# The adaLN modulation as fp32 products with the weights stationary, spread over the first norm and the mLSTM stages

## The reference, cut to what matters

```python
def trunk_layer(x, cond, li, P, rope, ctx):
    mod = jax.nn.silu(cond) @ P['w_mod'][li] + P['b_mod'][li]      # (1024) @ (1024 x 6144)
    sh1, sc1, g1, sh2, sc2, g2 = jnp.split(mod[:, None, :], 6, axis=-1)
    h = rms_norm(x, P['norm1'][li]) * (1 + sc1) + sh1
    mo, new_ctx = even_mixer(...) if li % 2 == 0 else odd_mixer(...)
    x = x + g1 * mo
    h = rms_norm(x, P['norm2'][li]) * (1 + sc2) + sh2
    x = x + g2 * swiglu(h, P['w_ffn_in'][li], P['w_ffn_out'][li])
```

## Time and profile before

| | us |
|---|---|
| runs | 3986.44, 3990.02, 3990.70 |
| median | 3990.02 |
| span of the profiled execution (no other time was kept of it) | 3988.1 |
| busy: TensorE, VectorE, ScalarE, GpSimd | 3424, 1966, 1161, 1820 |
| modulation | 8.9 to 159.2 |
| first norm, up to the first product of the projection | 159.2 to 206.3 |
| projection | 206.3 to 578.9 |
| gates | 578.9 to 642.0 |
| query and key stage | 642.0 to 679.2 |
| scan | 679.2 to 820.4 |
| output stage | 820.4 to 854.0 |
| all that follows | 854.0 to 3988 |

### The profile page before, as it was taken

One profiled execution on the slowest core, in us unless ns is written; L12 is line 12 of the kernel. 1 busy time (PEld: TensorE's weight loads), 2 busy tenths in 40 slices (PEclk: granted clock), 3 DMA queues, 4 the chain that ended last, 5 costly groups with the idle time before them and its releaser, 6 DMA issues. The chain is left out here.

```text
span 3988.1 us, 52620 instructions
## 1 busy us (share of the span) xinstructions
PE 3424.4 (86%) x17646; PEld 2961.2 (74%) x17646; DVE 1966.0 (49%) x3464; ACT 1161.0 (29%) x2474; POOL 1820.2 (46%) x1700
## 2 busy tenths in 40 slices
PE   7789993647768799999999686888888799999998
PEld 2377873536666699999998574777777699999998
DVE  7764115677772433333333675888883433333333
ACT  5611001146650310110110313888870310110110
POOL 0053102536551245545545354888871245545545
PEclk9899996859998899999999796999999899999999
DMA  8612212020002111110110212000002110110111
GB/s 331 253 69 98 87 45 77 5 94 17 15 7 90 50 44 34 53 42 32 53 42 1 103 61 78 17 16 16 18 1 90 53 43 32 53 42 32 53 42 48
DMA packets 118990, 232.74 MB, mean 58 GB/s; under 512 B 64064, under 2 KB 71360, under 8 KB 108736
## 3 DMA queue, kind: packets, MB, share of 16 engines
q1 hardware_dynamic: 118880, 231.33, 17.0%
HBM read 197.74 MB, written 34.34 MB: 58 GB/s over the span
## 5 line engine op out<-in xcount | busy, mean ns | idle before, releaser
L812 POOL TENSOR_TENSOR x<-x,ff_gated 128x512 f32<-128x512 f32 x396 | 512.1, 1293 | 320.1 <-DVE ff_gated L897 296.6
L806 POOL TENSOR_TENSOR ff_lo<-ff_raw,ff_hi 128x1024 fp32r<-128x1024 f32 x132 | 329.0, 2499 | 547.2 <-ACT ff_hi L773 547.0
L897 DVE TENSOR_TENSOR ff_gated<-ff_y_banks,gate_tokens 128x512 f32<-128x512 f32 x396 | 273.8, 691 | 412.6 <-PE ff_y_banks L871 411.2
L610 PE MATMUL tile_sum<-w_hi,tokens_hi 128*128 128x512 f32 x1008 | 405.1, 402 | 68.5 <-DVE w_lo L641 45.0
L773 ACT ACTIVATE ff_hi<-ff_raw 128x1024 fp32r<-128x1024 f32 x132 | 137.9, 1061 | 1118.7 <-PE ff_y_banks L871 720.5
L886 DVE TENSOR_TENSOR ff_silu<-ff_silu,ff_up_banks 128x384 f32<-128x384 f32 x132 | 72.5, 550 | 718.2 <-PE ff_up_banks L842 718.2
L611 PE MATMUL tile_sum<-w_lo,tokens_hi 128*128 128x512 f32 x1008 | 403.0, 400 | 0.0
L612 PE MATMUL tile_sum<-w_hi,tokens_lo 128*128 128x512 f32 x1008 | 402.3, 399 | 0.0
L838 PE MATMUL ff_gate_banks<-tokens_hi,ff_hi 128*128 128x384 f32 x1056 | 354.6, 336 | 19.4 <-POOL ff_lo L806 19.4
L839 PE MATMUL ff_gate_banks<-tokens_lo,ff_hi 128*128 128x384 f32 x1056 | 354.1, 335 | 0.0
L839 PE MATMUL ff_up_banks<-tokens_lo,ff_hi 128*128 128x384 f32 x1056 | 353.2, 334 | 0.0
(11 more groups left out here) (254 smaller groups left out, 7481.8 us busy)
## 6 DMA issues: line engine op xcount, KB each, us to landing
ff_raw<-in_w_ffn SPq DMA_DIRECT2D x132, 512.0 KB, 3.5
mod_raw<-in_w_mod SPq DMA_DIRECT2D x48, 1024.0 KB, 6.9
scratch_mixer_in<-tile_out SPq DMA_DIRECT2D x90, 256.0 KB, 2.0
w_raw<-in_w_in_even SPq DMA_DIRECT2D x14, 1024.0 KB, 6.4
q_double<-scratch_mixer_in SPq DMA_DIRECT2D x72, 128.0 KB, 2.3
w_raw<-in_w_in_odd SPq DMA_DIRECT2D x6, 1024.0 KB, 6.6
x<-in_x SPq DMA_DIRECT2D x9, 512.0 KB, 7.4
q_double<-scratch_mixer_in SPq DMA_DIRECT2D x72, 64.0 KB, 2.0
```

Of the source, the lines that this page charges most:

```text
L610: nc.tensor.matmul(acc, self.hi[:, k, mine], w_hi, start=(k == 0), stop=False)
L806: pool.tensor_tensor(lo[:, u], raw[:, slot], hi[:, u].bitcast(F32), ALU.subtract).then_inc(lo_done, 1)
L812: pool.tensor_tensor(self.x[:, t, cols], self.x[:, t, cols], y[:, m % YB], ALU.add).then_inc(added, 1)
```

## The change

The block `modulation` goes. The weights are laid out anew, as 48 pieces of 256 columns with all 1024 rows, and a piece is used as it was loaded, in fp32, as the stationary operand: 128 columns at a time, with the two silu columns moving, eight matmuls into two columns of one bank, `mod_sums`. So the result comes out as columns. A class `ModulationPieces` keeps a ring of slots, loads pieces on SP and multiplies `blocks` half pieces on TensorE where it is called:

- first norm: 8 pieces (all that this norm's shift and scale need), three slots, ahead of the transposes; loads behind x, ahead of the projection weights. ScalarE's squares and VectorE's normalising of the third group of tiles are put ahead of the wait for the sums.
- gates: 12 pieces, four slots, between the gate product and the transposes.
- query and key stage: three pieces, a half behind the scores at each of tiles 3 to 8; four loads behind tile 2, three behind tile 8.
- scan: 18 pieces, a half behind the turning of r and a half behind the update in each turn; loads behind the loading of the state. The loop over turns is unrolled.
- output stage: seven pieces, one behind the transposes of each of tiles 0 to 6; the last three loads behind the gate of tile 3. VectorE forms the other sums and scales at the end.

`tokens_hi` and `tokens_lo` are each two buffers of four column blocks, of which the first pair is freed between gates and attention to make room.

```diff
+    class ModulationPieces:
+        def load(self, sync, end):
+            w = self.program.t["w_mod"]
+            for i in range(self.n_loads, min(end, self.end)):
+                n = i - self.first
+                if n >= self.slots:
+                    sync.wait_ge(self.used, n - self.slots + 1)
+                sync.dma_start(self.raw[:, n % self.slots], w[i // MOD_PIECES, i % MOD_PIECES]).then_inc(self.loaded[n % self.slots], 16)
+            self.n_loads = max(self.n_loads, min(end, self.end))
+        def multiply(self, pe, acc, blocks):
+            for _ in range(blocks):
+                i, b = self.n_used, self.half
+                n = i - self.first
+                if b == 0:
+                    pe.wait_ge(self.loaded[n % self.slots], 16 * (n // self.slots + 1))
+                out = acc[:, i // MOD_PIECES, 2 * (i % MOD_PIECES) + b]
+                for k in range(KB):
+                    at = k * 256 + b * P
+                    mm = nc.tensor.matmul(out, self.raw[:, n % self.slots, at:at + P], silu[:, k], start=(k == 0), stop=(k == KB - 1))
+                if b == 1:
+                    mm.then_inc(self.used, 1)
+                    self.n_used += 1
+                self.half = 1 - b
+    def finish_modulation(self, acc, layer, a, b):
+        return nc.vector.tensor_tensor(self.mod[layer][:, a:b], acc[:, layer, a:b], bias[:, :, None].broadcast_to([P, b - a, 2]), ALU.add)
...
# norm
                         for t in range(NT):
                             sync.dma_start(x[:, t], self.t["x"][:, t]).then_inc(loaded[t], 16)
+                        pieces.load(sync, MOD_FIRST)
...
+                    if first:
+                        squares(groups[2])
+                        act.wait_ge(mod_own, 2)
                     scale_and_shift(0)
...
+                    if first:
+                        normalise(2)
+                        dve.wait_ge(pieces.used, MOD_FIRST)
+                        self.finish_modulation(acc, 0, 0, 2 * MOD_FIRST).then_inc(mod_own, 1)
+                        dve.wait_ge(mod_own, 1)
+                        self.norm_scales(0, 0).then_inc(mod_own, 1)
                     split_parts(0)
...
+                    if first:
+                        pieces.multiply(pe, acc, 2 * MOD_FIRST)
                     for n, (t0, cnt, k) in enumerate(items):
...
# mlstm_gates
                     sync.dma_start(wg[:], self.t["w_gates"]).then_inc(loaded, 16)
+                    pieces.load(sync, MOD_FIRST + 12)
...
                     mm.then_inc(product, 1)
+                    pieces.multiply(pe, acc, 24)
                     pe.wait_ge(act_own, 3)
...
# mlstm, queries and keys
+        A0, A1, A2, A3 = MOD_FIRST + 12, MOD_FIRST + 15, MOD_FIRST + 33, 2 * MOD_PIECES
                         sync.dma_start(vv[:, t, :, 0:W], src[5, t].rearrange("p (h e) -> p h e", h=H)).then_inc(v_loaded, 16)
+                        if t == 2:
+                            pieces.load(sync, A0 + 4)
+                    pieces.load(sync, A0 + 7)
                     sync.wait_ge(v_loaded, 16 * NT)
...
                             scores(t - 1)
+                        if t > 2:
+                            pieces.multiply(pe, acc, 1)
...
# mlstm, scan
                     sync.dma_start(CT[:], self.t["state"]).then_inc(state_in, 16)
+                    pieces.load(sync, A2 + 4)
...
                             turn_r(*nxt)
+                        pieces.multiply(pe, acc, 1)
...
                         mm.then_inc(upd_done, 1)
+                        pieces.multiply(pe, acc, 1)
...
# mlstm, output
                         sync.dma_start(og[:, t % RING], src[6, t]).then_inc(o_loaded[t % RING], 16)
+                        if t == RING - 1:
+                            pieces.load(sync, A3)
...
                     low(NT - 1)
+                    dve.wait_ge(pieces.used, A3 - A0)
+                    self.finish_modulation(acc, 0, 2 * MOD_FIRST, 48).then_inc(mod_own, 1)
+                    self.finish_modulation(acc, 1, 0, 48).then_inc(mod_own, 1)
+                    dve.wait_ge(mod_own, 2)
+                    for layer, which in ((0, 1), (1, 0), (1, 1)):
+                        self.norm_scales(layer, which).then_inc(mod_own, 1)
...
                         mm.then_inc(turned, 1)
+                        if pieces.n_used < A3:
+                            pieces.multiply(pe, acc, 2)
+                    pieces.multiply(pe, acc, 2 * (A3 - pieces.n_used))
```

More of the change, by code:

```diff
@@ L165, in _ @@
                     pool.memset(self.minus_one[:], -1.0)
-    def modulation(self):
-        nc = self.nc
[L173 to L301, removed]
-                        with pe.Fori(1, MOD_CHUNKS // 2) as r:
-                            for c in range(2):
-                                body(layer, r * 2 + c, c, True)
-                        turn((layer + 1) * MOD_CHUNKS - 1, MOD_CHUNKS - 1, 1)
@@ new lines, with __init__ @@
+    class ModulationPieces:
+        def __init__(self, program, stack, name, slots, first, end):
+            self.program, self.slots, self.first, self.end = program, slots, first, end
+            self.raw = program.sb(stack, name, [P, slots, 2048])
+            self.loaded = [program.sem(f"{name}_loaded{i}") for i in range(slots)]
+            self.used = program.sem(f"{name}_used")
+            self.n_loads = self.n_used = first
+            self.half = 0
+        def load(self, sync, end):
[7 more added lines that the diff above has]
+        def multiply(self, pe, acc, blocks):
+            nc = self.program.nc
+            silu = self.program.silu_cond[:].rearrange("p (c k) -> p k c", c=2)
+            for _ in range(blocks):
[11 more added lines that the diff above has]
+                self.half = 1 - b
@@ new lines, in finish_modulation, with norm_scales @@
+    def finish_modulation(self, acc, layer, a, b):
+        nc = self.nc
+        bias = self.par("b_mod")[:, layer * 48 + a:layer * 48 + b]
+        return nc.vector.tensor_tensor(self.mod[layer][:, a:b], acc[:, layer, a:b], bias[:, :, None].broadcast_to([P, b - a, 2]), ALU.add)
+    def norm_scales(self, layer, which):
+        nc = self.nc
+        gain = self.par(("norm1", "norm2")[which])[:, layer * KB:(layer + 1) * KB]
+        return nc.vector.scalar_tensor_tensor(out=self.norm_scale[layer][which][:], in0=self.mod[layer][:, 24 * which + 8:24 * which + 16, :],
+                                              scalar=1.0, in1=gain[:, :, None].broadcast_to([P, KB, 2]), op0=ALU.add, op1=ALU.mult)
@@ L317, in start, with norm @@
                 sync.dma_start(self.raw[:, i], source).then_inc(self.loaded[i], 16)
-    def norm(self, layer, which, gate_out=None, ahead=None):
+    def norm(self, layer, which, gate_out=None, ahead=None, mod_sums=None):
         nc = self.nc
@@ L374, in _ @@
                     squares(groups[1])
+                    if first:
+                        squares(groups[2])
+                        act.wait_ge(mod_own, 2)
                     scale_and_shift(0)
-                    squares(groups[2])
+                    if not first:
+                        squares(groups[2])
                     scale_and_shift(1)
@@ L2046, in add @@
                         pool.wait_ge(h_turn, n + 1)
-                        if not (isinstance(n, int) and n == 0):
+                        if not (n == 0):
                             pool.wait_ge(h_done, n)
```

112 lines of the change are left out of this document (61 added, 51 removed).

## The result

| | median of the runs, us | runs |
|---|---|---|
| before | 3990.21 (3985.72 to 3998.67) | 8 |
| after | 4004.47 (4002.15 to 4030.08) | 8 |

The ratio is 1.0044, with a 95% interval from 1.0027 to 1.0061: the change made the kernel slower by 0.44%. The prediction was 3924 us, with a range from 3886 to 3958. The profiled execution has a span of 4002.3 us in a run of 4004.14.

A forecast was written before the change was run, and what follows sets the result against it. The last chain to end lies far behind the change, so it acts only through the stages it touches: -125 + 5 + 16 + 22 + 16 = -66, a span of 3922; with the runs' median 1.9 us higher, 3924 us, range 3886 to 3958.

The forecast's parts named there:

- the price of one product: All stages with new products: a pass costs 0.11 us at either clock level, 3.52 us a piece, 169 us in all.
- far bound: Highest price considered for a new product's pass: 0.213 us, from a pass with 129 moving columns at 1.2 GHz.
- Modulation and first norm: Start of the kernel: the modulation block goes, eight pieces take 28.2 us, the end moves from 201.7 to 76.7, -125 us.
- Gates: Gates: twelve pieces between gate product and transposes take 42.2 us, longer than the wait they fill, +5 us.
- The cover of 36.8 us: Gates: time before the transposes in which new products could run free; short by 5 us for twelve pieces.
- Query and key stage: Query and key stage: tile 3 delayed 8.7 us behind weight loads, half pieces in six tiles add 7, +16 us.
- the hole before tile 3: Query and key stage: a hole of 9 us before tile 3's keys, which stand behind four weight loads.
- Scan: Scan: half pieces cost nothing at full clock, 2.2 us a turn at 1.2 GHz; middle taken, +22 us (3 to 38).
- Output stage: Output stage: seven pieces behind the transposes, tiles 0 to 2 at 4.6 us each, tile 4's gate late, +16 us.
- a pass costs 0.213 us: Rival, all stages with products: fp32 weight loads are slow at 1.2 GHz; +105 us, 4095 us, slower; chance 0.09.
- the products keep the clock up: Rival, all stages with products: they count as activity and close TensorE's pauses; 3896 us; chance 0.17.
- Theory A: From the experiments: fp32 passes cost 0.107 us at full clock, 0.213 at half; stretches of two-column products run at half.

The follow-up runs named there:

- k8: The changed kernel with the 54 transposes in the gates written as plain matmuls with the identity moving; 4034.05 us in one run.
- k2: The changed kernel with only 36 of the 128 rows multiplied in each new product; 4086.5 us in one run.
- k1: The changed kernel with 128 moving columns in each new product, the two silu columns repeated 64 times; 3902.44 us, 0.9772 of the kernel before.
- k3: The changed kernel with one of every eight new products made, all loads kept; 3871.4 us in one run.
- k5: The changed kernel with 128 moving columns and weight loads spread over tiles in the query and key and output stages; 3889.23 us, 0.9747 of the kernel before.

## Why the prediction was wrong

The step that failed is the price of one product: "Since few columns move I take 0.11 us at either level". Measured it is 0.107 at full clock and 0.21 at half, 0.207 on average over the gates, and passes over 0.13 us were the text's own sign of being wrong. The text had this price as its far bound, and as the condition of its rival, and set it aside because of L1878. That row was a transpose, as the rival said; k8 shows that as a product it has twice the records at twice the price each, and k2 that its few rows had no part in it. L275, the other row, was at full clock and right for that level alone. With a price that was the same at both levels, the text had no reason to ask what the clock does to the products themselves, in the norm, the gates and the output stage. It did say that in the clock's view the products look like a pause, and the gates bear it out, from 1.00 to 0.50 with TensorE busy; but it drew on this for the scan's own matmuls alone.

By its steps:

- *Modulation and first norm*, -125, measured -100.0. The products took 54.5 us instead of 28.2, which is the whole difference. The loads, the squares ahead, and the split of 1.06 us a pair held: with wide products (k1) the step gives -123.4.
- *Gates*, +5, measured +42.5. The cover of 36.8 us stood as read; 79.34 us were laid in it instead of 42.2. In k1, with 43.05, the stage loses 4.5.
- *Query and key stage*, +16, measured +14.4. The mechanism was right: the hole before tile 3 came (k3 shows it with the products nearly gone) and grew to 12.69 us from 1.48, so by 11.2 where 8.7 was predicted; with the products at full clock the tiles behind it then stood 3.5 us apart (612.95 to 616.45), as the text had it for that level, so that they added some 3 us where it took 7. The two misses partly cancel, and the full clock was that of this profile: k8, with the same instructions in this stage, took 67.7 us. k5, which has wide products and spreads the loads, has +9.7.
- *Scan*, +22, measured +23.9. The sum is right by chance. A turn at half clock costs 12.83 us and not 9.7, since its two halves take 6.6 us and not 3.5, and one at full clock 6.69, under the 7.5 of before, where the text let it cost nothing.
- *Output stage*, +16, measured +35.5: 7.6 us a tile instead of 4.6. The wait for tile 4's gate is there, 2.30 us of it with the slow products and 5.60 in k1.

Those misses are 25.0 + 37.5 - 1.6 + 1.9 + 19.5 - 1.5 (projection) - 0.5 (behind) = 80.3, from a span of 3922 to the 4002.3 measured.

The rival "a pass costs 0.213 us" had the norm at -99, the gates at +45 and the output stage at +35: measured -100.0, +42.5 and +35.5. It missed the query stage and the scan (30 and 94 against 14.4 and 23.9), because it took half clock throughout, and these ran at 0.78 and 0.74. So it came out at 4095 instead of 4004, with the right sign. The rival "the products keep the clock up" comes near k1 and k5 (3896 against 3902 and 3889), but not near this change, whose products have two columns. Two small slips change nothing here: that rival's terms add up to -95, not -94, and the far bound, 1.72 us for eight passes, is 0.215. The Trainium skill, "TensorE: Matmul & The Clock Gate", section "Why this matters for your kernels", asks for TensorE to be kept busy without gaps; the gates of after had no gap in 79.30 us and stood at 0.52, so the trace does not bear out that rule for these products, as the prediction said of it.

Left open is why the clock of narrow products mixed with other matmuls differs so much: in the query and key stage between profiles (0.52 to 0.78), in the scan of after from turn to turn (0.50 and 1.00). Theory A covers stretches of such products alone. Open too is whether the rows matter to the clock, as k2 suggests, and what in the wide form keeps it up: k1 changed the count of moving columns, the operand's pattern and the columns written together.

## What to carry to other kernels

A price taken from a neighbouring row has to come from the same kind of instruction at the same clock: a transpose says nothing of a product, and a row at full clock nothing of a stage at half. Where an edit puts small fp32 products into a stage that TensorE spent waiting, price them at half clock and see what is then late. Where two columns and 128 cost nearly the same, as here (0.107 and 0.112 us a pass at full clock), moving more columns is nearly free, and repeating two columns to 128 turned a loss of 0.44% into a gain of 2.3%, and with the loads spread 2.5%.

## What the runs showed of the hardware

- A pass of a plain fp32 product with 128 stationary columns took 0.205 to 0.215 us at half clock with 2, 36 or 129 moving columns (after, k8), and 0.107 at full clock with 2, 0.112 with 128 (after, k1).
- Back to back, products of two moving columns ran 79.30 us at a granted clock of 0.52, having begun at 1.00; those of 128 ran 42.90 us at 1.00, with TensorE busy throughout in both.
- In the first norm the clock's record does not tell the clock. In after it says 1.00 beside passes 0.214 us apart, as in the gates at half clock (the line of after). In k1 it says 1.00 in both of two stretches of the same products, with 9 records in 2.00 us in one and 20 in the other.

```profile
25.00:79.50 54.50, 54.47 (x256) 54.47 (x257) 2.74 (x4) 0.00 (x0) 0.00 (x0) 1.00 0.45 166
```

```profile
26.00:28.00 2.00, 2.00 (x9) 2.00 (x10) 2.00 (x4) 0.00 (x0) 0.00 (x0) 1.00 1.01 422
30.00:32.00 2.00, 2.00 (x20) 2.00 (x20) 0.00 (x0) 0.00 (x0) 0.00 (x0) 1.00 0.01 4
```
